# Second query projection in the joined 512-column form, with the memory's normalised halves made step by step beside it

## What is computed

```python
def _memory_cross_attn(h, mem_n, w_q, w_kv, w_o):
    q = (h @ w_q).reshape(bsz, seq, XA_HEADS, XA_HEAD_DIM)
    k, v = jnp.split(mem_n @ w_kv, 2, axis=-1)
    ...
    s = jnp.einsum("bshd,bmhd->bhsm", q.astype(f32), k.astype(f32)) * (XA_HEAD_DIM ** -0.5)
    p = jax.nn.softmax(s, axis=-1)
    o = jnp.einsum("bhsm,bmhd->bshd", p, v.astype(f32)).reshape(bsz, seq, D_MODEL)
    return o.astype(h.dtype) @ w_o
...
x = x + _memory_cross_attn(_rmsnorm(x, xa_norm[i]), _rmsnorm(mem, xa_mem_norm[i]),
                           xa_w_q[i], xa_w_kv[i], xa_w_o[i])
```

## Time and profile before

| | |
|---|---|
| median of 3 runs | 1285.88 us |
| lowest, highest | 1285.85, 1286.6 us |
| profiled execution: its own time | 1285.5 us |
| profiled execution: its span | 1283.7 us |
| TensorE busy | 1273.2 us (99% of the span) |
| VectorE busy | 998.1 us (78%) |
| ScalarE busy | 762.5 us (59%) |
| POOL busy | 237.1 us (18%) |
| matmuls | 8074 |

### The profile page before, as it was taken

One profiled execution on the slowest core, in us unless ns is written; L12 is line 12 of the kernel. 1 busy time (PEld: TensorE's weight loads), 2 busy tenths in 40 slices (PEclk: granted clock), 3 DMA queues, 4 the chain that ended last, 5 costly groups with the idle time before them and its releaser, 6 DMA issues.

```text
span 1283.7 us, 23539 instructions
## 1 busy us (share of the span) xinstructions
PE 1273.2 (99%) x8074; PEld 1153.8 (90%) x8074; DVE 998.1 (78%) x1549; ACT 762.5 (59%) x1378; POOL 237.1 (18%) x311
## 2 busy tenths in 40 slices
PE   9999999999999999999999999999999999999997
PEld 8888888899999888888888888999999989888887
DVE  6888778897668888668888668998887767888854
ACT  7655554555556556545556447878865656555643
POOL 2433110122002111111111112024421201111111
PEclk9999999999999999999999999999999999999999
DMA  8556645655435556645556647654445544555661
GB/s 282 187 182 211 205 159 173 196 186 175 154 134 187 188 191 210 206 162 167 192 183 225 197 147 263 223 158 132 133 135 197 184 160 137 181 189 185 225 195 51
DMA packets 63095, 232.52 MB, mean 181 GB/s; under 512 B 7024, under 2 KB 8112, under 8 KB 62896
## 3 DMA queue, kind: packets, MB, share of 16 engines
q1 hardware_dynamic: 62368, 230.73, 54.7%
q10 hardware_dynamic: 656, 0.86, 0.2%
HBM read 230.49 MB, written 1.08 MB: 180 GB/s over the span
## 4 chain that ended last, share of the span: by engine, by line
PE 96%; DVE 2%; ACT 1%; issue 0%; DMA 0%; POOL 0%; ACTq 0%; DVEq 0%
PE bank L1440 95%; DVE w_lo L831 1%; DMA raw<-w_gu 0%; PE bank L1788 0%; PE bank L1600 0%; PE bank L1760 0%; DVE t L831 0%; ACT w_hi L405 0%; PE bank L1540 0%; PE bank L1815 0%; DVE acc L831 0%; ACT gate L458 0%; DVE final L1335 0%; DVE y L831 0%; DVE rms_n L834 0%
## 5 line engine op out<-in xcount | busy, mean ns | idle before, releaser
L831 DVE TENSOR_TENSOR w_lo<-raw,w_hi 128x1024 fp32r<-128x1024 f32 (+2 forms) x403 | 524.0, 1303 | 42.8 <-ACT w_hi L405 41.7
L405 ACT ACTIVATE w_hi<-raw 128x1024 fp32r<-128x1024 f32 (+2 forms) x403 | 441.8, 1098 | 35.4 <-PE bank L1440 27.8
L1440 PE MATMUL bank<-h,w_hi 128*128 128x512 f32 (+1 forms) x1808 | 447.1, 385 | 0.9 <-DVE h L834 0.6
L1440 PE MATMUL bank<-a,w_hi 128*128 128x256 f32 (+1 forms) x1878 | 386.7, 324 | 0.4 <-DVE w_lo L831 0.2
L1440 PEld LDWEIGHTS bank<-h,w_hi 128*128 128x128 f32 x1808 | 321.3, 189 | 54.9 <-DVE h L834 1.2
L1440 PEld LDWEIGHTS bank<-a,w_hi 128*128 128x128 f32 x1878 | 310.8, 190 | 24.9 <-issue 0.6
L1440 PE MATMUL bank<-a,w_lo 128*128 128x256 f32 x1280 | 260.6, 283 | 0.0
L1440 PEld LDWEIGHTS bank<-h,w_lo 128*128 128x128 f32 x1736 | 242.1, 190 | 16.7
L1440 PE MATMUL bank<-h,w_lo 128*128 128x256 f32 x1736 | 254.7, 282 | 0.0
L405 ACT ACTIVATE corr<-bank 128x256 f32<-128x256 f32 x239 | 91.1, 382 | 267.2 <-PE bank L1440 267.2
L1440 PEld LDWEIGHTS bank<-a,w_lo 128*128 128x128 f32 x1280 | 204.5, 191 | 4.8
(11 more groups left out here) (201 smaller groups left out, 1064.3 us busy)
## 6 DMA issues: line engine op xcount, KB each, us to landing
raw<-w_gu SPq DMA_DIRECT2D x174, 512.0 KB, 4.1
raw<-w_down SPq DMA_DIRECT2D x64, 704.0 KB, 4.2
raw<-w_xbc SPq DMA_DIRECT2D x32, 512.0 KB, 3.9
raw<-w_conv_in SPq DMA_DIRECT2D x24, 512.0 KB, 3.5
raw<-w_q SPq DMA_DIRECT2D x16, 512.0 KB, 4.1
raw<-w_k SPq DMA_DIRECT2D x16, 512.0 KB, 3.5
raw<-w_v SPq DMA_DIRECT2D x16, 512.0 KB, 3.5
raw<-w_o SPq DMA_DIRECT2D x16, 512.0 KB, 4.0
```

What stands on the lines that cost most here:

```text
L405: return nc.scalar.activation(out, in_, ACT.Copy, scale=scale)
L831: return nc.vector.tensor_tensor(out, a, b, op)
L1440: return nc.tensor.matmul(out, lhs, rhs, start=start, stop=stop, skip_group_check=check)
```

## The change

q1 gets the joined form: `project` and the table of joined phases name it, and `attention` of ScalarE and VectorE drop the branches by layer, so that the second layer does what the first does: eight `corr_copy` on ScalarE, and `q_sum` with a scaling in place on VectorE. `Q_SCALED` gets a count for the second layer. The memory's pieces 0 and 1 are no longer made in the opening but in step 1, and piece s in step s for s from 2 to 7: on ScalarE between `corr_copy` and the rounding, on VectorE at the end of the step, behind the split. The wait for the memory's load moves with piece 0.

```diff
--- before.py
+++ after.py
@@ -251,13 +251,13 @@
 
         FFN_A = {0: 0, 1: FT + KT + KT, 2: 2 * FT + 2 * KT, 3: 3 * FT + 3 * KT}
         KV_PARTS = KT + 4
-        CONV_SCALED, Q_SCALED = 0, KT - 1
+        CONV_SCALED, Q_SCALED = 0, {0: KT - 1, 1: 2 * KT - 1}
         CONV_A, Q_A = FT, {0: FT + KT, 1: 3 * FT + 2 * KT}
 
         X_COUNT = {n: KT * i for i, n in enumerate(("down0", "conv_out", "down1", "down2", "down3"))}
         pair_first, pair_count = {}, 0
         for name, units, _ in PHASES:
-            if name[:4] == "down" or name[:2] == "gu" or name in ("conv_in", "q0"):
+            if name[:4] == "down" or name[:2] == "gu" or name in ("conv_in", "q0", "q1"):
                 pair_first[name] = pair_count
                 pair_count += KT if name in X_COUNT else units - (name == "conv_in")
             if name == "down2":
@@ -567,21 +567,15 @@
             def attention(layer):
                 n0 = first[f"q{layer}"]
                 for s in range(25):
-                    if s != 1 and (layer or s != 2):
+                    if s not in (1, 2):
                         split(n0 + s + AHEAD)
                     if s == 24:
                         break
                     if s == 0:
-                        if layer == 0:
-                            corr_copy(0, 0, n0)
-                        else:
-                            act.wait_ge(mem_in, 64 + 16 * layer)
-                            new_mem(layer, 0)
-                            new_mem(layer, 1)
+                        corr_copy(0, 0, n0)
                         split(n0 + 1 + AHEAD)
-                        if layer == 0:
-                            corr_copy(1, 1, n0 + 1)
-                            split(n0 + 2 + AHEAD)
+                        corr_copy(1, 1, n0 + 1)
+                        split(n0 + 2 + AHEAD)
                         norm(2 if layer == 0 else 6)
                     for h in range(HEADS):
                         if s == 11 + 2 * h:
@@ -590,15 +584,14 @@
                                 nc.scalar.activation(probs[h][:, tt, :], bank[5][:, tt * 256:tt * 256 + 256], ACT.Exp,
                                                      bias=neg_mx[:, tt:tt + 1], accum_out=tot[:, tt:tt + 1]).then_inc(exp_ready, 1)
                     if s < KT:
-                        if layer == 0:
-                            if s > 1:
-                                corr_copy(s % 4, s, n0 + s)
-                            act.wait_ge(scaled_ready, Q_SCALED + s + 1)
-                        else:
-                            if s + 2 < KT:
-                                new_mem(layer, s + 2)
-                            b, use = bank_use(f"q{layer}", s)
-                            act.wait_ge(evac[b], use + 1)
+                        if s > 1:
+                            corr_copy(s % 4, s, n0 + s)
+                        if layer and s:
+                            if s == 1:
+                                act.wait_ge(mem_in, 64 + 16 * layer)
+                                new_mem(layer, 0)
+                            new_mem(layer, s)
+                        act.wait_ge(scaled_ready, Q_SCALED[layer] + s + 1)
                         copy(a_hi[:, KT + s, :], t2[s % 2][:, :]).then_inc(ahi_ready, 1)
                     elif s < 2 * KT:
                         b, use = bank_use(f"k{layer}", s - KT)
@@ -1055,45 +1048,38 @@
                 rest_of(a_lo[:, 2 * h:2 * h + 2, :], value_bank(h)[:, :].rearrange("p (a n) -> p a n", a=2),
                         a_hi[:, 2 * h:2 * h + 2, :]).then_inc(o_ready, 1)
 
-            def q_sum(t):
-
-                at_least(dve, a_ready, Q_A[0] + t - 1)
-                joined("q0", t, t2[t % 2][:, :])
+            def q_sum(layer, t):
+
+                at_least(dve, a_ready, Q_A[layer] + t - 1)
+                joined(f"q{layer}", t, t2[t % 2][:, :])
 
             def attention(layer):
                 n0 = first[f"q{layer}"]
                 for s in range(24):
                     if s == 0:
                         split(n0 + AHEAD)
-                        for k in range(2 * layer):
-                            mem_rest(layer, k)
                         norm(2 if layer == 0 else 6)
-                        if layer == 0:
-                            q_sum(0)
+                        q_sum(layer, 0)
                         split(n0 + 1 + AHEAD)
-                        if layer == 0:
-                            q_sum(1)
+                        q_sum(layer, 1)
                         dve.wait_ge(rms_ready, SS_INDEX[2 if layer == 0 else 6] + 1)
                     for h in range(HEADS):
                         if s == 11 + 2 * h:
                             softmax_max(layer, h)
                     if s < KT:
                         b, use = bank_use(f"q{layer}", s)
-                        if layer == 0:
-                            if s > 1:
-                                q_sum(s)
-                            dve.wait_ge(evac[b], use + 1)
-                            tt(t2[s % 2][:, :], t2[s % 2][:, :], rms_k[:, :]).then_inc(scaled_ready, 1)
-                        else:
-                            dve.wait_ge(unit_done, n0 + s + 1)
-                            at_least(dve, a_ready, Q_A[layer] + s - 1)
-                            tt(t2[s % 2][:, :], bank[b][:, 0:SEQ], rms_k[:, :]).then_inc(evac[b], 1)
-                        if layer == 0 and s == 1:
+                        if s > 1:
+                            q_sum(layer, s)
+                        dve.wait_ge(evac[b], use + 1)
+                        tt(t2[s % 2][:, :], t2[s % 2][:, :], rms_k[:, :]).then_inc(scaled_ready, 1)
+                        if s == 1:
                             split(n0 + 2 + AHEAD)
-                        if s > (1 if layer else 2):
+                        if s > 2:
                             split(n0 + s + AHEAD)
-                        if layer and s + 2 < KT:
-                            mem_rest(layer, s + 2)
+                        if layer and s:
+                            if s == 1:
+                                mem_rest(layer, 0)
+                            mem_rest(layer, s)
                     elif s < 2 * KT:
                         k = s - KT
                         dve.wait_ge(unit_done, n0 + s + 1)
@@ -1578,7 +1564,7 @@
                             one_unit(n0 + 2 * t + u, out, half, u * half, a, u == 0, u == 1)
 
             def project(name, b, tiles=KT):
-                joined = name in ("conv_in", "q0")
+                joined = name in ("conv_in", "q0", "q1")
                 opening(pair_unit if joined else unit, name, b)
                 for t in range(4, tiles):
                     one_unit = pair_unit if joined and t < 3 * KT - 1 else unit
```

## The result

The changed kernel takes 1291.87 us (median of 6 runs, 1291.27 to 1292.52) against 1285.87 us before: 6.0 us more, a ratio of 1.0046 (95% interval 1.0036 to 1.0057). The profiled execution has a span of 1290.7 us against 1283.7 us. The forecast was 1290.1 us, its range ended at 1291.4. The direction and the waits came out as forecast; the time lies above the range.

A forecast was written before the change was run, and what follows sets the result against it. TensorE's instruction stream was taken to bound the kernel. Shorter matmuls (-0.62 us) plus TensorE's waiting (4.8 us) gave +4.2 us on 1285.9, so 1290.1 us, range 1288.0 to 1291.4.

The forecast's parts named there:

- The matmuls' gain: Second query phase, TensorE: eight units change to the joined form, 23.68 to 23.06 us, saving 0.62 us.
- VectorE's schedule: Second query phase: VectorE takes 2.81 us a step from step 3 on, so mn_lo(7) ends at +30.36.
- the ring's corr copy: Query phase: ScalarE's corr(s), in a loop through VectorE's sum and scaling and ScalarE's copy and split, 2.66 us around.
- The waits: TensorE waits 4.8 us: about 0.8 before unit 6, 1.5 before key block 6, 2.5 before block 7.
- After that TensorE has no reason to wait: Behind key block 7: other engines have drained their steps, key steps are as before; no further waiting.
- a rival with 0.08 and 1293.0 us: TensorE's clock falls to 1.2 GHz behind the new gaps for one unit's work: +2.9 us more, chance 0.08.
- the rival of the ring's pace: Second query phase: steps follow the 2.66 us loop through ScalarE and VectorE; net +2.1 to +3.3 us, chance 0.18.
- The rival on the other side: Second query phase: VectorE is not late, only the shorter matmuls count; not slower, 1285.3 us, chance 0.06.

The follow-up runs named there:

- the last kernel: Changed kernel with memory pieces 0 to 4 before the norm, 5 to 7 in step 2, k_lo(1) ahead of VectorE's split in both key phases: 1284.80 us, ratio 0.9994.
- the kernel with only the 2.2 us gap: Changed kernel plus 11 unused matmuls filling the wait before piece 6, the wait before piece 7 left unfilled: 1291.44 us, ratio 1.0043.

## Why the prediction was wrong

*The matmuls' gain.* Right: -0.62 us forecast; 23.05 against 23.68 us for the phase once no wait stands in it, and 0.61 us up to the value phase in the last kernel.

*VectorE's schedule.* Right, step by step. Forecast and found, in us after the phase's first matmul: q_sum(3) +16.22 and +16.21, q_sum(7) +27.46 and +27.44, mn_lo(7) from +29.40 and +29.36, block 7 on TensorE +30.4 and +30.36. The step of 2.81 us, made from a row of before and one sum, is what the trace shows. It came out because the first query phase was a measured model of the second, and because 0.88 us for mn_lo was taken from the row with POOL beside it; the kernel with mn_lo first shows the other price. In the earlier trace rows VectorE's wait before a sum is put down to POOL, not to the ring's corr copy. The kernel with mn_lo first settles it: there POOL's subtraction of 1002.15 ends at 1003.74, behind the sum's start at 1003.39, and the pace is the same 2.66 us.

*The waits.* Right: 4.8 us in three pieces, 0.8, 1.5 and 2.5. The profile's waits, 0.79, 1.23 and 2.17, are idle time only. Measured as lateness of block 7 it is 30.36 - 25.58 = 4.78.

*"After that TensorE has no reason to wait", and nothing lost later.* Right for the waits of the changed kernel. But the sum -0.62 + 4.8 takes it that nothing is lost behind the waits, and this is the step that failed: what TensorE's own idle time does to its clock stood in the sum at nothing. It was named as a rival with 0.08 and 1293.0 us. The trace of before could not have shown it, since its longest wait is 1.1 us; a mean row of 1.00 where TensorE is never idle is no evidence for what happens where it is. What the runs showed in its place: the clock fell to half in the wait before piece 7, at a cost of 2.46 us in the profile (2.30 when it was run again) and about 2 us in the medians. 1285.9 + 4.2 + 2.0 = 1292.1, measured 1291.87. The rival had the right mechanism and a price that was too high, 2.9 us: it doubled the time of one unit, while the rows show blocks of 0.64 for 0.36 us, 1.8 times as long, over 5.9 us of work. Giving it 8% on the strength of rows that could not speak to it was the mistake. Had the range reached to that rival, it would have held the time.

The Trainium skill (TensorE: Matmul & The Clock Gate, HAM oscillation) describes a TensorE that idles between bursts and starts the next one at half clock. The trace agrees in kind: 0.50 from 1014 on. But the idle gaps that the Trainium skill names there are longer than any single wait forecast or found here, so the prediction read more into it than it says. The measurement decides: in the kernel with only the 2.2 us gap that shorter gap was enough.

*The ranges.* The rival of the ring's pace is given as +2.1 to +3.3 us, but the bounds worked out for it end at a net +2.7; 3.3 us is the waiting from which the matmuls' 0.62 had yet to be taken. The stated range does not hang on it.

*The rival on the other side*, a VectorE that isn't late, fell: the lateness is there in every kernel with the joined form. *The ring's pace* is real, 2.66 us a step, where mn_lo stands ahead of the split or outside these steps; with mn_lo behind the split it is hidden under the 2.81 us of VectorE's own work.

*Two things that the forecast passed over* are small here and showed only in the variants: lateness of VectorE reaches the scores behind key unit 2 (0.67 us with the pieces in their old places, 0.27 us with them hidden; in the changed kernel no such wait is left, since TensorE itself comes later), and POOL's subtraction can catch a split too (1.76 us).

## What to carry to other kernels

Here one engine bounds the kernel and is almost never idle. A helper's lateness costs such a kernel nothing as long as buffers cover it. It costs its full length at the first instruction whose result is wanted at once. So before you move work to the end of a helper's steps, compute at what time the last step ends, not how much idle time it has on average. A measured sibling phase in the same trace gave that time to within 0.1 us here. Where a change brings TensorE a new wait of some 2 us, count the slow stretch behind it too, and test that part with matmuls that only fill the gap.

## What the runs showed of the hardware that was not expected

A single wait of 2.2 us between stretches of full work let the granted clock go from 2.4 to 1.2 GHz in most executions of that kernel (four of five by their spans). In the profiled one it fell over 1 us after TensorE had begun to work again. With a wait of 1.2 us and 0.36 us of work ahead of the 2.2 us, it fell already within the second wait, in both profiles and, by the times, in all eleven executions. The clock then stayed low for about 3.4 us of work in the first kernel and 5.5 to 5.9 us in the second. At the lower clock a block of three matmuls took 0.64 us instead of 0.36. Waits of 0.8 and 1.3 us, and in the kernel with mn_lo first of 1.6 and 1.1 us nine microseconds apart, left it at 1.00 in the profiles.
